# Sparse attention: turning and value products one step later, coefficients ahead of the masked minima

## The chip, the cores and the metric

One core of a Trainium2 chip. The metric is the device time of one launch in microseconds (us). The engines are PE (TensorE, matrix products and transposes, into the eight PSUM banks), DVE (VectorE), ACT (ScalarE), POOL (GpSimd) and SP, which here only issues the loads. Each engine works through its own program in order, and they meet by semaphores.

## The reference, cut to what matters

Two transformer layers, a third block with context, and an expert layer, for 256 tokens of width 1024. The change lies in the sparse attention of the second layer (`nsa_mixer`): 16 heads of width 64 in 4 key groups, three branches. With 256 tokens there are only four blocks of 64 keys, so the branch that selects blocks takes all of them, and the window of 256 holds every earlier key. Two branches are therefore plain causal attention over 256 keys, each with its own keys and values:

```python
ss = jnp.einsum('bqgrd,bgqkd->bgrqk', qb, k_sel)
p_slc = masked_softmax(ss, sel_mask)
o_slc = jnp.einsum('bgrqk,bgqkd->bqgrd', p_slc.astype(v_sel.dtype), v_sel)
sw = jnp.einsum('bqgrd,bkgd->bgrqk', qb, k_win)
p_win = masked_softmax(sw, win_mask)
o_win = jnp.einsum('bgrqk,bkgd->bqgrd', p_win.astype(v_win.dtype), v_win)
out = gb[..., 0:1] * o_cmp + gb[..., 1:2] * o_slc + gb[..., 2:3] * o_win
```

The third branch, over 15 compressed keys, is made before the loop; its product with its values is added inside it.

## The kernel before, in words

All weights stream through a ring of six raw tiles of 1 MB; ACT copies each to a high part (`make_high`, L407), POOL subtracts to get the low part (L421), and PE multiplies three times for each product (L480, L481, L482). Nearly the whole kernel is such products.

The attention takes 16 steps (`NS`): eight pairs of heads by two branches, `steps[n] = (c, br)`. One step n goes through these stations:

- scores(n), PE, L1773: eight products of queries and keys into banks 4 and 5. It waits for `masked` of step n - 1, which says that the banks have been read.
- minima(n), DVE, L2035: four operations that add the causal mask, write to buffer `SB[n % 4]` and leave the row minimum of the negated scores. The last sets `masked`.
- exps(n), ACT, L1894: four exponentials in place in SB, with their row sums. They wait for `masked` of n.
- coefs(n), DVE, L2017 and L2019: the reciprocal of the sums, and its product with the gate. They wait for the exponentials of n.
- scale(n), POOL, L1673: four multiplications of SB by the coefficient, after coefs(n). Before it POOL makes, in steps 2 to 13, a quarter of a weight tile's low part (L444).
- turn(n), PE, L1801: six transposes of SB into banks 6 and 7. It waits for scale(n), and for both copies of turn n - 1.
- copies(n): ACT (L1921) takes bank 6 to `PT[n % 2]`, DVE (L2044) bank 7. They wait for turn(n) and for values(n - 2).
- values(n), PE, L1818: eight products with the values; in even steps L1811 goes ahead (the compressed branch, two products).

The order on each engine is written out by hand. The first three scores, minima and exponentials lie beside the projection of the values (`between` at L1789), which ends with a wait of PE for all of its products (`flush`, L1790). Then the loops run: PE at n does scores(n), turn(n - 2), values(n - 3); DVE does minima(n), coefs(n - 1), its copy(n - 2); ACT does exps(n), its copy(n - 2), and makes a high part of a weight tile ahead of the exponentials at n = 3 and n = 8; after its copy it splits finished outputs (`o_high`, L1910) at n = 8, 12, 16, and DVE (`o_low`, L2024) at n = 9, 13, 17. After the loop PE goes on with the output projection (`cols_product`, L1830), whose tiles are ready.

Of the kernel before, what the change touches and what calls it, by code (L numbers as in the profile page):

```python
# [20 lines left out]
ACT = mybir.ActivationFunctionType  # L21
# [95 lines left out]
class Modulation:  # L117
# [37 lines left out]
    def turn(self, pe, j, bank, row):  # L155

        pe.wait_ge(*self.copied.at(j + 1))
        for c in range(4):
            last = self.k.nc.tensor.matmul(bank[:, 2 * c:2 * c + 2], row[:, c * P:(c + 1) * P], self.pick, start=True, stop=True)  # L159
        last.then_inc(self.turned.sem, 1)  # L160
# [111 lines left out]
class Kernel:  # L272
# [1324 lines left out]
    def nsa(self):  # L1597
# [3 lines left out]
        nc, ps, G = self.nc, self.psum, G_NSA  # L1601
        v_, s_ = nc.vector, nc.scalar
# [25 lines left out]
        PT = [work(f"PT{i}", 768).rearrange("p (b n) -> p b n", b=2) for i in range(2)]  # L1628
# [10 lines left out]
        sco, masked, sexp, scoef, sscale, stn, spa, spd, spv, ohigh, olow = self.counters(  # L1639
            "at_scores", "at_masked", "at_exp", "at_coef", "at_scaled", "at_turned", "at_PT_act", "at_PT_dve", "at_values",  # L1640
            "at_o_high", "at_o_low")
# [7 lines left out]
        NS = len(steps)  # L1649
# [28 lines left out]
        def _(pe):  # L1678
# [84 lines left out]
            def scores(n):  # L1763
                c, br = steps[n]
                if n:
                    pe.wait_ge(*masked.at(n))
                else:
                    pe.wait_ge(*fd.at(20))
                    pe.wait_ge(*rready.at(1))
                for t in range(TT):  # L1770
                    for b in range(2):
                        rows = slice(64 * b, 64 * b + 64)
                        last = nc.tensor.matmul(ps[4 + b][:, 0:P] if t == 0 else ps[4 + b][:, P:384],  # L1773
                                                qT[rows, c, t * P:(t + 1) * P], kT[br][rows, c // 4, 0:(t + 1) * P],
                                                start=True, stop=True)
                last.then_inc(sco.sem, 1)
# [15 lines left out]
            def turn(n):  # L1792
                pe.wait_ge(*sscale.at(n + 1))
                if n:
                    pe.wait_ge(*spa.at(n))
                    pe.wait_ge(*spd.at(n))
                else:
                    pe.wait_ge(*cpte.at(1))
                for b in range(2):
                    for j in range(3):  # L1800
                        last = nc.tensor.transpose(ps[6 + b][:, j * P:(j + 1) * P], SB[n % 4][:, b, j * P:(j + 1) * P], self.ident)  # L1801
                last.then_inc(stn.sem, 1)

            def values(n):
                c, br = steps[n]
                o = ps[c // 2][:, (c % 2) * T:(c % 2 + 1) * T]
                if n == 0:
                    pe.wait_ge(*vbd.at(2))
                    pe.wait_ge(*vready.at(2))
                if br == 0:  # L1810
                    nc.tensor.matmul(o, Vbd[:, c // 4, 2 * (c % 4):2 * (c % 4) + 2, :].rearrange("p h d -> p (h d)"),  # L1811
                                     cPT[:, c // 4, :], start=c % 2 == 0, stop=True, skip_group_check=True)
                pe.wait_ge(*spa.at(n + 1))
                pe.wait_ge(*spd.at(n + 1))
                for t in range(TT):
                    for b in range(2):
                        col = br * 256 + (2 * (c // 4) + b) * 64
                        last = nc.tensor.matmul(o[64 * b:64 * b + 64, t * P:T], vv[:, t, col:col + 64],  # L1818
                                                PT[n % 2][:, b, 0:T] if t == 0 else PT[n % 2][:, b, T:384],
                                                start=False, stop=True, skip_group_check=True)  # L1820
                last.then_inc(spv.sem, 1)

            for n in range(2, NS + 3):
                if 3 <= n < NS:
                    scores(n)
                if 2 <= n < NS + 2:
                    turn(n - 2)
                if n >= 3:
                    values(n - 3)
            self.cols_product(pe, G, 16, self.xT, KD, 4, olow)  # L1830

        @self.block.scalar
        def _(act):
# [53 lines left out]
            def exps(n):  # L1887
                act.wait_ge(*masked.at(n + 1))
                if n >= 4:
                    act.wait_ge(*scoef.at(n - 3))  # L1890
                for b in range(2):
                    for t, cut in enumerate((slice(0, P), slice(P, 384))):
                        w = SB[n % 4][:, b, cut]
                        last = s_.activation(w, w, ACT.Exp, scale=-1.0, bias=nm[n % 4][:, 2 * t + b:2 * t + b + 1],  # L1894
                                             accum_out=sums[n % 4][:, 2 * t + b:2 * t + b + 1])
                last.then_inc(sexp.sem, 1)
# [10 lines left out]
            def o_high(j):  # L1907
                act.wait_ge(*spv.at(4 * j + 4))
                for k in (2 * j, 2 * j + 1):
                    s_.activation(self.xT[0][:, k, :], ps[j][:, (k % 2) * T:(k % 2 + 1) * T], ACT.Copy).then_inc(ohigh.sem, 1)  # L1910

            for n in range(NS + 2):
                if n in (3, 8):
                    self.make_high(act, G + 16 + (n + 2) // 5)
                if 3 <= n < NS:
                    exps(n)
                if n >= 2:
                    act.wait_ge(*stn.at(n - 1))
                    if n >= 4:
                        act.wait_ge(*spv.at(n - 3))  # L1920
                    s_.activation(PT[n % 2][:, 0, :], ps[6][:, 0:384], ACT.Copy).then_inc(spa.sem, 1)  # L1921
                if n >= 8 and n % 4 == 0:
                    o_high(n // 4 - 2)
            o_high(3)
# [4 lines left out]
        def _(dve):  # L1929
# [82 lines left out]
            def coefs(n):  # L2012
                c, br = steps[n]
                dve.wait_ge(*sexp.at(n + 1))
                if n >= 4:
                    dve.wait_ge(*sscale.at(n - 3))
                link(v_.reciprocal(coef[n % 4], sums[n % 4]))  # L2017
                o = coef[n % 4].rearrange("p (t b) -> p t b", t=TT)
                v_.tensor_tensor(o, o, gates[:, :, 2 * c:2 * c + 2, 1 + br], ALU.mult).then_inc(scoef.sem, 1)  # L2019

            def o_low(j):
                dve.wait_ge(*ohigh.at(2 * j + 2))
                for k in (2 * j, 2 * j + 1):
                    v_.tensor_tensor(self.xT[1][:, k, :], ps[j][:, (k % 2) * T:(k % 2 + 1) * T],  # L2024
                                     self.xT[0][:, k, :].bitcast(F32), ALU.subtract).then_inc(olow.sem, 1)

            for n in range(NS + 2):
                if n < NS:
                    dve.wait_ge(*sco.at(n + 1))
                    if n >= 4:  # L2030
                        dve.wait_ge(*stn.at(n - 3))
                        dve.wait_ge(*sexp.at(n - 3))
                    for b in range(2):
                        for t, cut in enumerate((slice(0, P), slice(P, 384))):
                            last = v_.tensor_tensor_reduce(SB[n % 4][:, b, cut], ps[4 + b][:, cut], causal[:, cut], -SC, 3.0e38,  # L2035
                                                           ALU.add, ALU.min, nm[n % 4][:, 2 * t + b:2 * t + b + 1])
                    last.then_inc(masked.sem, 1)
                if 1 <= n < NS + 1:
                    coefs(n - 1)
                if n >= 2:  # L2040
                    dve.wait_ge(*stn.at(n - 1))
                    if n >= 4:
                        dve.wait_ge(*spv.at(n - 3))
                    v_.tensor_copy(PT[n % 2][:, 1, :], ps[7][:, 0:384]).then_inc(spd.sem, 1)  # L2044
                if n >= 9 and n % 4 == 1:
                    o_low(n // 4 - 2)
            o_low(3)
# [1280 lines left out]
```

## Time and profile before

| | us |
|---|---|
| median of three runs | 2133.19 |
| lowest, highest | 2129.83, 2133.97 |
| the profiled execution | 2131.12 |
| its span | 2129.3 |
| PE busy in the span | 2100.2 (99%) |
| POOL busy | 1654.5 (78%) |
| ACT busy | 1116.4 (52%) |
| DVE busy | 880.1 (41%) |
| TensorE's granted clock | 0.998 of full speed |

Rows of the timeline give the start in us from the beginning of the span, the busy time, the engine, the line of the kernel, the operation and its operands; in brackets stands the idle time before it and what the profile takes to have ended it. An instruction's busy time can overlap the start of the next one on the same engine, so the distance of two starts is what one costs in a row of work.

### The profile page before, as it was taken

To read this page: it belongs to the slowest core of one execution; us is meant where nothing else is said; L and a number is where in the kernel's file an instruction comes from. 1 tells how busy PE (TensorE), PEld (TensorE's weight loads), DVE (VectorE), ACT (ScalarE), POOL (GpSimd) and SP (SyncE) were. 2 spreads that over 40 slices of the span, in tenths; PEclk is the share of its full clock that TensorE was granted. 3 is DMA by queue.
4 is the path that set the end of the run, shared out by engine and by line. 5 is a ranking of instruction groups with operands and counts; after the bars stand their busy time and mean duration, and the time that the engine had idled before them with its cause. 6 is when DMAs were issued, how large, how long until landed. Compare 5 with 4: busy or idle time off the path is not lost.

```text
span 2129.3 us, 39500 instructions
## 1 busy us (share of the span) xinstructions
PE 2100.2 (99%) x15948; PEld 1972.1 (93%) x15948; DVE 880.1 (41%) x1921; ACT 1116.4 (52%) x1784; POOL 1654.5 (78%) x811
## 2 busy tenths in 40 slices
PE   9999999999999998999999999999999999999998
PEld 9999889999999986999989999999999998888886
DVE  6114633114112434411746315997667512322224
ACT  6455765435444446544654545555554455555555
POOL 5887667887888556888766576797676789999997
PEclk9999999999999999999999999999999999999999
DMA  8555666556555431655453355355444455555554
GB/s 306 198 181 195 258 237 257 197 197 251 196 197 186 170 139 62 219 181 196 177 191 139 139 178 208 110 191 167 140 149 140 149 177 195 197 194 196 191 196 149
DMA packets 77586, 393.70 MB, mean 185 GB/s; under 512 B 10749, under 2 KB 11901, under 8 KB 46849
## 3 DMA queue, kind: packets, MB, share of 16 engines
q1 hardware_dynamic: 77440, 391.70, 52.1%
q8 instruction: 99, 1.62, 0.3%
q14 instruction: 47, 0.38, 0.1%
HBM read 390.62 MB, written 1.05 MB: 184 GB/s over the span
## 4 chain that ended last, share of the span: by engine, by line
PE 84%; DVE 2%; ACT 1%; POOL 1%; issue 1%; DMA 0%; ACTq 0%; SPq 0%; DVEq 0%; POOLq 0%
PE bank L480 25%; PE bank L482 25%; PE bank L481 25%; PE bank L960 3%; PE bank L2717 3%; POOL nsa_SB L1673 1%; DMA ring_raw<-in_stream 0%; PE bank L1773 0%; PE bank L1801 0%; PE bank L147 0%; PE bank L1818 0%; DVE nsa_SB L2035 0%; PE bank L159 0%; DVE keep_red L2424 0%; ACT ring_high L407 0%
## 5 line engine op out<-in xcount | busy, mean ns | idle before, releaser
L421 POOL TENSOR_TENSOR ring_low<-ring_raw,ring_high 128x2048 fp32r<-128x2048 f32 x204 | 944.1, 4640 | 330.4 <-ACT ring_high L407 329.5
L2677 POOL TENSOR_TENSOR peerS_low<-peerS_raw,peerS_high 128x512 fp32r<-128x512 f32 x510 | 662.8, 1319 | 113.0 <-ACT peerS_high L2821 111.2
L480 PE MATMUL bank<-keep_xThigh,ring_high 128*128 128x256 f32 x2112 | 591.9, 280 | 5.0 <-POOL ring_low L421 1.5
L481 PE MATMUL bank<-keep_xTlow,ring_high 128*128 128x256 f32 x2112 | 585.7, 277 | 0.0
L482 PE MATMUL bank<-keep_xThigh,ring_low 128*128 128x256 f32 x2112 | 585.6, 277 | 0.0
L407 ACT ACTIVATE ring_high<-ring_raw 128x2048 fp32r<-128x2048 f32 x207 | 396.8, 1917 | 279.8 <-PE bank L482 247.6
L2821 ACT ACTIVATE peerS_high<-peerS_raw 128x512 fp32r<-128x512 f32 x510 | 319.5, 627 | 175.3 <-PE bank L482 150.4
L480 PEld LDWEIGHTS bank<-keep_xThigh,ring_high 128*128 128x128 f32 x2112 | 397.6, 188 | 13.5 <-issue 6.6
L481 PEld LDWEIGHTS bank<-keep_xTlow,ring_high 128*128 128x128 f32 x2112 | 398.0, 188 | 0.4
L482 PEld LDWEIGHTS bank<-keep_xThigh,ring_low 128*128 128x128 f32 x2112 | 397.8, 188 | 0.0
L480 PE MATMUL bank<-keep_xThigh,peerS_high 128*128 128x256 f32 x1024 | 292.0, 285 | 0.1
L481 PE MATMUL bank<-keep_xTlow,peerS_high 128*128 128x256 f32 x1024 | 285.9, 279 | 0.0
L482 PE MATMUL bank<-keep_xThigh,peerS_low 128*128 128x256 f32 x1024 | 285.7, 279 | 0.0
L921 DVE TENSOR_TENSOR bank<-bank,keep_R 128x512 f32<-128x512 f32 x44 | 30.8, 700 | 423.7 <-PE bank L482 423.5
L3043 DVE TENSOR_TENSOR peerS_GAlow<-peerA_A,peerS_GAhigh 128x256 fp32r<-128x256 f32 x127 | 98.2, 774 | 245.3 <-ACT peerS_GAhigh L2846 245.3
L480 PE MATMUL bank<-peerS_high,peerS_GAhigh 128*128 128x512 f32 x508 | 197.7, 389 | 0.6 <-DVE peerG_GA3low L3043 0.6
L481 PE MATMUL bank<-peerS_low,peerS_GAhigh 128*128 128x512 f32 x508 | 197.6, 389 | 0.0
L482 PE MATMUL bank<-peerS_high,peerS_GAlow 128*128 128x512 f32 x508 | 197.6, 389 | 0.0
L480 PEld LDWEIGHTS bank<-keep_xThigh,peerS_high 128*128 128x128 f32 x1024 | 193.1, 189 | 0.6 <-PE bank L960 0.2
L481 PEld LDWEIGHTS bank<-keep_xTlow,peerS_high 128*128 128x128 f32 x1024 | 193.6, 189 | 0.0
L482 PEld LDWEIGHTS bank<-keep_xThigh,peerS_low 128*128 128x128 f32 x1024 | 192.9, 188 | 0.0
L480 PEld LDWEIGHTS bank<-peerS_high,peerS_GAhigh 128*128 128x128 f32 x508 | 95.3, 188 | 20.7 <-DVE peerG_GA3low L3043 1.0
(549 smaller groups left out, 3546.8 us busy)
## 6 DMA issues: line engine op xcount, KB each, us to landing
ring_raw<-in_stream SPq DMA_DIRECT2D x237, 1024.0 KB, 4.8
peerS_raw<-in_experts SPq DMA_DIRECT2D x256, 512.0 KB, 3.7
start_x<-in_x SPq DMA_DIRECT2D x2, 512.0 KB, 4.0
ring_raw<-in_stream SPq DMA_DIRECT2D x4, 256.0 KB, 5.5
context_in<-in_ctx SPq DMA_DIRECT2D x1, 1024.0 KB
mix_band_band<-in_band SPq DMA_DIRECT2D x1, 1024.0 KB, 7.4
peerT_keys_keys<-in_stream SPq DMA_DIRECT2D x1, 1024.0 KB, 4.8
out<-keep_x SPq DMA_DIRECT2D x4, 256.0 KB, 2.2
```

The lines of the kernel that those rows point to most:

```text
L407: self.nc.scalar.activation(self.parts(n)[0], self.raw_slot(n), ACT.Copy).then_inc(self.high_done.sem, 1)
L421: self.nc.gpsimd.tensor_tensor(low_, self.raw_slot(n), high.bitcast(F32), ALU.subtract).then_inc(self.low_done.sem, 1)
L480: mm(out, sh, mh, start=start, stop=False)
L481: mm(out, sh, ml, start=False, stop=False)
L482: return mm(out, sl, mh, start=False, stop=stop)
L921: v_.tensor_tensor(pair(i, 0), pair(i, 0), over, ALU.mult).then_inc(scaled.sem, 1)
L960: ins = self.nc.tensor.matmul(out, lhsT, rhs, start=start, stop=stop)
L1673: last = g_.tensor_scalar(w, w, coef[n % 4][:, 2 * t + b:2 * t + b + 1], 1.0, ALU.mult, ALU.mult)
L2677: g_.tensor_tensor(low[:, m % 2, cut], xraw[:, m % 3, cut], high[:, m % 2, cut].bitcast(F32), ALU.subtract).then_inc(made_low.sem, 1)
L2717: last = nc.tensor.matmul(ps[2 + q % 2][:, j * P:(j + 1) * P], O1[:, o, :], O2[:, o, :], start=True, stop=True)
L2821: s_.activation(halves_of(m, 0)[:, cut], xraw[:, m % 3, cut], ACT.Copy).then_inc(made_high.sem, 1)
L3043: v_.tensor_tensor(cell(1, n), A[:, n, :], cell(0, n).bitcast(F32), ALU.subtract).then_inc(gal.sem, 1)
```

## The change

The loop of PE runs scores(n), turn(n - 3), values(n - 4), from n = 3 to NS + 3. ACT runs exps(n), copy(n - 3), from n = 3. DVE runs coefs(n - 1) first, then minima(n), then copy(n - 3). The buffers, the instructions of each station, their number, and POOL's program stay as they are. The first turn, which stood ahead of scores(3), now stands behind it.

```diff
-            for n in range(2, NS + 3):
-                if 3 <= n < NS:
+
+            for n in range(3, NS + 4):
+                if n < NS:
                     scores(n)
-                if 2 <= n < NS + 2:
-                    turn(n - 2)
-                if n >= 3:
-                    values(n - 3)
+                if n < NS + 3:
+                    turn(n - 3)
+                if n >= 4:
+                    values(n - 4)
...
-            for n in range(NS + 2):
+            for n in range(3, NS + 3):
                 if n in (3, 8):
                     self.make_high(act, G + 16 + (n + 2) // 5)
-                if 3 <= n < NS:
+                if n < NS:
                     exps(n)
-                if n >= 2:
-                    act.wait_ge(*stn.at(n - 1))
-                    if n >= 4:
-                        act.wait_ge(*spv.at(n - 3))
-                    s_.activation(PT[n % 2][:, 0, :], ps[6][:, 0:384], ACT.Copy).then_inc(spa.sem, 1)
+                m = n - 3
+                act.wait_ge(*stn.at(m + 1))
+                if m >= 2:
+                    act.wait_ge(*spv.at(m - 1))
+                s_.activation(PT[m % 2][:, 0, :], ps[6][:, 0:384], ACT.Copy).then_inc(spa.sem, 1)
...
-            for n in range(NS + 2):
+            for n in range(NS + 3):
+                if 1 <= n < NS + 1:
+                    coefs(n - 1)
                 if n < NS:
                     dve.wait_ge(*sco.at(n + 1))
...
                     last.then_inc(masked.sem, 1)
-                if 1 <= n < NS + 1:
-                    coefs(n - 1)
-                if n >= 2:
-                    dve.wait_ge(*stn.at(n - 1))
-                    if n >= 4:
-                        dve.wait_ge(*spv.at(n - 3))
-                    v_.tensor_copy(PT[n % 2][:, 1, :], ps[7][:, 0:384]).then_inc(spd.sem, 1)
+                if n >= 3:
+                    m = n - 3
+                    dve.wait_ge(*stn.at(m + 1))
+                    if m >= 2:
+                        dve.wait_ge(*spv.at(m - 1))
+                    v_.tensor_copy(PT[m % 2][:, 1, :], ps[7][:, 0:384]).then_inc(spd.sem, 1)
```

## Rows read from the trace of the kernel before

**Rows 1.** Waits of PE over the span: engine line waited for: us, times, longest.
```profile
PE bank L1801 <- POOL nsa_SB L1673: 7.8, 10, 1.4
```

**Rows 2.** Windows: the loop from scores(4) to scores(15), busy time of each engine.
```profile
792.78:828.28 35.50, 29.54 (x254) 19.47 (x253) 24.21 (x126) 26.81 (x103) 31.29 (x55) 1.00 0.17 61
```

**Rows 3.** Timeline of PE: scores(10), turn(9), values(8), scores(12), turn(11).
```profile
812.71 0.93 PE L1773 MATMUL bank<-nsa_kT,nsa_qT 64*128 64x128 f32 x8
...
817.25 0.85 PE L1801 MATMUL bank<-keep_ident,nsa_SB 128*128 128x128 f32 x6 [1.16 <-POOL nsa_SB L1673]
...
818.46 0.87 PE L1818 MATMUL bank<-nsa_PT,nsa_vv 128*64 128x256 f32 x8
819.26 0.93 PE L1773 MATMUL bank<-nsa_kT,nsa_qT 64*128 64x128 f32 x8
...
823.81 0.85 PE L1801 MATMUL bank<-keep_ident,nsa_SB 128*128 128x128 f32 x6 [1.16 <-POOL nsa_SB L1673]
```

**Rows 4.** Timeline of POOL: scale(9), a quarter, scale(11).
```profile
815.27 1.63 POOL L1673 TENSOR_SCALAR nsa_SB<-nsa_SB,nsa_coef 128x128 f32<-128x128 f32 x4 [0.96 <-DVE nsa_coef L2019]
816.87 1.27 POOL L444 TENSOR_TENSOR ring_low<-ring_raw,ring_high 128x512 fp32r<-128x512 f32 x1
...
821.82 1.63 POOL L1673 TENSOR_SCALAR nsa_SB<-nsa_SB,nsa_coef 128x128 f32<-128x128 f32 x4 [0.68 <-DVE nsa_coef L2019]
```

**Rows 5.** Timeline of ACT: first of exps(10), copy(8), copy(10).
```profile
814.92 0.40 ACT L1894 ACTIVATE nsa_SB<-nsa_SB,nsa_nm 128x128 f32<-128x128 f32 x1 [1.65 <-DVE nsa_nm L2035]
...
816.69 0.47 ACT L1921 ACTIVATE nsa_PT<-bank 128x384 f32<-128x384 f32 x1
...
823.24 0.47 ACT L1921 ACTIVATE nsa_PT<-bank 128x384 f32<-128x384 f32 x1
```

**Rows 6.** Timeline of all engines: minima(15), turn(13), exps(15), coefs(15).
```profile
829.25 0.29 DVE L2035 CUSTOM_DVE_ANT_0 nsa_SB<-bank,nsac_causal 128x128 f32<-128x128 f32 x1 [0.50 <-PE bank L1773]
...
830.37 0.85 PE L1801 MATMUL bank<-keep_ident,nsa_SB 128*128 128x128 f32 x6 [1.16 <-POOL nsa_SB L1673]
...
830.49 0.40 ACT L1894 ACTIVATE nsa_SB<-nsa_SB,nsa_nm 128x128 f32<-128x128 f32 x1 [0.22 <-DVE nsa_nm L2035]
...
832.38 0.18 DVE L2017 RECIPROCAL nsa_coef<-nsa_sums 128x4 f32<-128x4 f32 x1 [0.58 <-ACT nsa_SB L1894]
```

**Rows 7.** Timeline of DVE: coefs(9)'s reciprocal, copy(8), the product of coefs(10).
```profile
814.80 0.17 DVE L2017 RECIPROCAL nsa_coef<-nsa_sums 128x4 f32<-128x4 f32 x1
...
815.09 0.55 DVE L2044 COPY nsa_PT<-bank 128x384 f32<-128x384 f32 x1
...
817.47 0.70 DVE L2019 TENSOR_TENSOR nsa_coef<-nsa_coef,nsa_gates 128x4 f32<-128x4 f32 x1
```

**Rows 8.** Timeline of ACT from the loop's start: copy(0), high part, exps(3), exps(4).
```profile
790.03 0.47 ACT L1921 ACTIVATE nsa_PT<-bank 128x384 f32<-128x384 f32 x1
790.40 1.90 ACT L407 ACTIVATE ring_high<-ring_raw 128x2048 fp32r<-128x2048 f32 x1
792.20 0.39 ACT L1894 ACTIVATE nsa_SB<-nsa_SB,nsa_nm 128x128 f32<-128x128 f32 x1
...
794.99 0.40 ACT L1894 ACTIVATE nsa_SB<-nsa_SB,nsa_nm 128x128 f32<-128x128 f32 x1 [0.56 <-DVE nsa_nm L2035]
```

**Rows 9.** Timeline of PE: turn(0), the first work behind the flush.
```profile
789.11 0.84 PE L1801 MATMUL bank<-keep_ident,nsa_SB 128*128 128x128 f32 x6 [0.30 <-POOL nsa_SB L1673]
```

**Rows 10.** Timeline from turn(14) to the output projection: turn, values(13), copy(14), turn(15), projection.
```profile
832.82 0.85 PE L1801 MATMUL bank<-keep_ident,nsa_SB 128*128 128x128 f32 x6 [0.38 <-POOL nsa_SB L1673]
...
833.60 0.87 PE L1818 MATMUL bank<-nsa_PT,nsa_vv 128*64 128x256 f32 x8
833.71 0.50 ACT L1921 ACTIVATE nsa_PT<-bank 128x384 f32<-128x384 f32 x1 [0.98 <-PE bank L1801]
...
834.54 0.88 PE L1801 MATMUL bank<-keep_ident,nsa_SB 128*128 128x128 f32 x6
...
837.23 0.38 PE L480 MATMUL bank<-keep_xThigh,ring_high 128*128 128x256 f32 x1
```

## The prediction

> **What bounds the kernel now.** The page comes first: PE is busy for 99% of the span, at full clock, so a change can only give back time in which PE stands idle. The list of PE's waits says where that is: the longest entry of the whole span is the turns of this attention, 7.8 us in ten waits, put down to POOL's scaling [rows 1]. The waits behind the attention are short handovers right behind PE's own work, which move along with PE; so what the loop loses or wins stays in the total. The window of the loop then gives the pace: 35.50 us from scores(4) to scores(15), eleven steps, 3.23 us each, with PE busy 29.54 of it [rows 2].
>
> Next the timeline of the loop, engine by engine, to see what a turn really waits for. The profile names POOL. Turn(9) starts at 817.25, scale(9) was over at 815.27 + 1.63 = 816.90, a gap of 0.35; turn(11) starts at 823.81, 0.36 behind scale(11) [rows 3, 4]. A turn also waits until ACT has emptied bank 6, and copy(8) ends at 816.69 + 0.47 = 817.16, copy(10) at 823.24 + 0.47 = 823.71, both 0.09 to 0.10 before the turns [rows 5]. So the turn is released by ACT's copy, and that copy is late because it is queued on ACT behind exps(n). The loop's period is this circle over two steps: scores(10) at 812.71; exps(10) at 814.92 (2.21: scores, minima); copy(8) at 816.69 (1.77: four exponentials); turn(9) at 817.25 (0.56); turn, compressed product and values until scores(12) at 819.26 (2.01). Together 6.55 us for two steps [rows 3, 5].
>
> **The change part by part.** No station gains or loses an instruction. Three things move.
>
> *Turn and values one step later.* PE at n + 1 now runs turn(n - 2) where it ran turn(n - 1). It waits for copy(n - 3), and ACT runs that copy behind exps(n), as copy(n - 2) before. The circle scores(n), minima(n), exps(n), copy, turn, values, scores(n + 2) keeps every member: 6.55 us for two steps. scale gets a step more of lead, but it was not what the turns waited for. Value in the loop: nothing.
>
> *coefs(n - 1) ahead of minima(n) on DVE.* coefs(n - 1) waits for all exponentials of n - 1, and those wait for the last minimum of n - 1. Before, this wait stood behind minima(n), and minima(n) could run beside exps(n - 1). Now what is queued behind the waiting instruction is minima(n), and for it wait exps(n) and, through `masked`, scores(n + 1). That closes a new circle over one step: from the first exponential to the reciprocal 832.38 - 830.49 = 1.89; from the reciprocal through the product to the next DVE operation 815.09 - 814.80 = 0.29; from the first minimum to the first exponential 830.49 - 829.25 = 1.24 [rows 6, 7]. Sum 3.42 us. No row has minima behind coefs; the nearest is the copy behind coefs, the 0.29. The minima wait for one semaphore more, so I take 0.03 more, 3.45, with 3.42 and 3.50 as ends. Two steps then take 6.90, more than the old circle's 6.55, so the new circle rules and the old one has 0.35 of slack in two steps. PE's work is hidden in it. The DVE copy and `o_low` lie in the 1.89 in which DVE waits for ACT.
>
> At n = 8 ACT makes a high part of a weight tile between its copy and the exponentials. From first exponential to copy 1.77, to the high part 790.40 - 790.03 = 0.37, through it 792.20 - 790.40 = 1.80: 3.94 instead of 3.45, so 0.49 more once [rows 5, 8].
>
> *The start.* PE's first work behind the flush starts at 789.11 [rows 9]; it is now scores(3) instead of turn(0), so exps(3) could start at 789.11 + 2.21 = 791.32. But ACT makes the high part first, now without copy(0) ahead of it: 790.03 + 1.80 = 791.83 [rows 8]. That rules. exps(4) follows at 791.83 + 3.45 = 795.28, against 794.99: 0.29 later.
>
> *The end.* From exps(4) to exps(15) it was 830.49 - 794.99 = 35.50; it becomes 11 x 3.45 + 0.49 = 38.44: 2.94 later [rows 6, 8]. From exps(15) to the output projection it was 837.23 - 830.49 = 6.74 [rows 6, 10]. Now one turn and one values more are left at that point. copy(12) runs at 1.77 after exps(15) begins, turn(13) at 1.77 + 0.56 = 2.33; turn(13), compressed product and values(12) take 2.01: 4.34; turn(14) 833.60 - 832.82 = 0.78 and values(13) 819.26 - 818.46 = 0.80: turn(15) at 5.92; from there to the projection 837.23 - 834.54 = 2.69: 8.61 [rows 3, 10]. copy(14) doesn't hold turn(15) up: it can begin 833.71 - 832.82 = 0.89 behind turn(14), at 5.23, and takes 0.50. scale(15) is over at 1.89 + 0.47 + 1.63 = 3.99 (the 0.47 from the reciprocal to scaling is 815.27 - 814.80) [rows 4, 7]. The tail is 8.61 - 6.74 = 1.87 longer.
>
> **Sum:** 0.29 + 2.94 + 1.87 = +5.1 us. The profiled execution took 2131.12 (span 2129.3 and 1.8 around it), so 2136.2 for its like. It lies 2.1 below the median of the runs, 2133.19; on the median the sum is 2138.3. That is what I predict.
>
> *A lock between DVE and POOL.* The product of coefs(10) took 0.70 us, where its fellows take 0.17, and ended at 818.17; POOL's quarter ran from 816.87 to 818.14 [rows 4, 7]. So it was held until the quarter was over. This matters more now, since coefs is on the circle. The Trainium skill has a rule for it (page "SBUF — State Buffer", section "SBUF: two separate sides"): VectorE operations with two SBUF inputs and GpSimd operations take a shared port as an exclusive lock for the whole instruction. By that rule any overlap would lengthen the circle, and the rival below prices it; the trace agrees by that row. Where does the quarter fall? Counted from the first exponential, scaling begins at 1.89 + 0.47 = 2.36, the quarter at 2.36 + 1.60 = 3.96, and it is over at 5.23; the next reciprocal begins at 3.45 + 1.89 = 5.34 [rows 4, 6]. It misses by 0.1, and since POOL starts from coefs the two stay in step. I take nothing for it; the upper end is 0.53 in each of ten steps, 5.3 us.
>
> **The rivals.**
> *B, the new circle is hidden.* If the minima were still released by their scores, the pace would stay 3.23 and only start and tail count: 0.29 + 1.87 = +2.2, 2135.4. For it: DVE idles much in the loop (24.21 of 35.50 busy, rows 2). Against it: exps(10) to coefs and minima is a strict order of waits.
> *C, the page is right and POOL is the bound; faster.* Turn(n - 3) finds its scaling long done and the 7.8 us of PE's waits go [rows 1]; less the tail, 7.8 - 1.9 = 5.9 us faster, 2127.3. It decides from the point where a step takes under 3.03 us: 0.29 + 11p - 35.50 + 1.87 = 0 gives p = 3.03. Against it: exponentials and minima alone, 1.89 + 1.24 = 3.13, stand above that, and the copies meet the turns to 0.1 us.
> *D, the lock.* Up to 5.3 us on top: 2143.6. For it the 0.70; against it the order worked out above.
> That the later turn doesn't do what it says is part of the forecast: the lead it gives to POOL goes unused, because the copy stays behind exps.
>
> **How the numbers follow.** Forecast 0.68, B 0.13, C 0.08, D 0.11. What a measurement tells from no change is about 0.2%, 4.3 us. The forecast's +5.1 lies just above; its own spread (3.42 to 3.50 a step is -0.3 to +0.6 us, and three runs before spread over 4.1 us) puts some 0.28 of it below: 0.49 slower, 0.19 within. With B within, D slower and C faster: slower 0.60, same 0.32, faster 0.08. The range 2133.5 to 2143.0 holds B, the forecast and most of D's smaller sizes, and leaves out C.
>
> **What would show it.** Right: DVE's reciprocals (L2017) idle before each for ACT, about 1.3 us in nearly every step (1.89 less the copy), where before one did; first exponentials 3.45 us apart; the quarters at n = 4 to 13 leave L2019 at 0.17; the projection starts near 842.3. Wrong: waits for PE's scores still ahead of the minima, or steps under 3.2 us; a step near 3.45 with the projection before 840 would mean that the tail is wrong.

## The result, and the profile after

| | before | changed |
|---|---|---|
| median, us (six runs each) | 2132.06 | 2140.84 |
| lowest, highest | 2129.83, 2133.97 | 2138.88, 2146.34 |
| ratio, 95% interval | | 1.0039, 1.0024 to 1.0054 |
| the profiled execution | 2131.12 | 2146.34 |
| PE's first work behind the flush to the projection | 48.12 | 56.91 |

The change makes the kernel slower, by 8.8 us on the medians; the forecast said 5.1. The profiled execution of the changed kernel is the slowest of its six, and 4.5 us of its distance lie ahead of the attention loop, where nothing was changed. Of these, 1.7 are a fall of TensorE's granted clock to 0.50 from 762.2 to 765.6, where the trace before stays at 1.00: from the first L960 product behind its wait of 0.49 us to the loop it is 793.62 - 760.38 = 33.24 against 789.11 - 757.57 = 31.54. So the stretch itself is the measure: from the first PE work behind the flush to the output projection. It was 789.11 to 837.23 [rows 9, 10] and is 793.62 to 850.53, 8.79 us longer.

PE's waits in the changed kernel. The turns are still on top, in place of the 7.8 us of [rows 1]. "issue" means that the profile shows no releaser; in all of them ACT's copy of the turn before ended 0.10 us ahead:

```profile
PE bank L1801 <- issue: 10.7, 11, 2.1
PE bank L1801 <- ACT nsa_PT L1922: 1.8, 1, 1.8
```

One step of the new circle (a closed chain of waits, in which each waits for the one before it), from the timeline of DVE and ACT: reciprocal, product, first minimum, first exponential, next reciprocal. It answers to [rows 6, 7].

```profile
827.90 0.18 DVE L2018 RECIPROCAL nsa_coef<-nsa_sums 128x4 f32<-128x4 f32 x1 [1.46 <-ACT nsa_SB L1895]
828.11 0.16 DVE L2020 TENSOR_TENSOR nsa_coef<-nsa_coef,nsa_gates 128x4 f32<-128x4 f32 x1
828.26 0.29 DVE L2038 CUSTOM_DVE_ANT_0 nsa_SB<-bank,nsac_causal 128x128 f32<-128x128 f32 x1
...
829.49 0.40 ACT L1895 ACTIVATE nsa_SB<-nsa_SB,nsa_nm 128x128 f32<-128x128 f32 x1 [1.25 <-DVE nsa_nm L2038]
...
831.39 0.18 DVE L2018 RECIPROCAL nsa_coef<-nsa_sums 128x4 f32<-128x4 f32 x1 [1.46 <-ACT nsa_SB L1895]
```

831.39 - 827.90 = 3.49 us, and DVE stands idle for 1.46 ahead of both reciprocals. Where the minima follow coefs the distance from the reciprocal to the next operation is 0.36, not the 0.29 + 0.03 that the forecast took. Now the first exponentials of steps 4, 5 and 15 ("step 4" is below the time from exps(4) to exps(5)):

```profile
799.98 0.40 ACT L1895 ACTIVATE nsa_SB<-nsa_SB,nsa_nm 128x128 f32<-128x128 f32 x1 [1.26 <-DVE nsa_nm L2038]
...
804.62 0.40 ACT L1895 ACTIVATE nsa_SB<-nsa_SB,nsa_nm 128x128 f32<-128x128 f32 x1 [2.41 <-DVE nsa_nm L2038]
...
840.32 0.40 ACT L1895 ACTIVATE nsa_SB<-nsa_SB,nsa_nm 128x128 f32<-128x128 f32 x1 [1.25 <-DVE nsa_nm L2038]
```

Step 4 takes 4.64 instead of 3.49, and the tail from exps(15) to the projection at 850.53 takes 10.21 instead of the 8.61 of the forecast. The reason stands in PE's timeline behind the two longest waits:

```profile
798.82 0.85 PE L1801 MATMUL bank<-keep_ident,nsa_SB 128*128 128x128 f32 x6 [2.06 <-issue]
...
800.23 1.55 PE L1818 MATMUL bank<-nsa_PT,nsa_vv 128*64 128x256 f32 x8
801.71 1.63 PE L1773 MATMUL bank<-nsa_kT,nsa_qT 64*128 64x128 f32 x8
...
842.65 0.85 PE L1801 MATMUL bank<-keep_ident,nsa_SB 128*128 128x128 f32 x6 [1.84 <-ACT nsa_PT L1922]
...
845.11 1.54 PE L1801 MATMUL bank<-keep_ident,nsa_SB 128*128 128x128 f32 x6
```

Eight values took 0.87 us before [rows 3] and take 1.55, eight scores 1.63 instead of 0.93. The windows give TensorE's granted clock (the third number from the end):

```profile
798.00:800.00 2.00, 1.18 (x8) 0.91 (x8) 1.59 (x11) 0.74 (x4) 1.15 (x3) 0.94 0.00 0
800.00:801.00 1.00, 1.00 (x5) 0.53 (x6) 0.42 (x1) 1.00 (x5) 1.00 (x3) 0.50 0.00 0
...
844.00:845.00 1.00, 1.00 (x8) 0.52 (x6) 0.09 (x1) 0.58 (x3) 0.31 (x1) 0.57 0.00 0
845.00:846.00 1.00, 1.00 (x6) 0.90 (x5) 0.00 (x0) 0.00 (x0) 0.00 (x0) 0.50 0.00 0
```

It fell to 0.50, its lower level of 1.2 GHz, and was back at 1.00 in the window from 804. A mean of 0.94 over two us means that it fell 0.24 us before 800.00, so at 799.8, about 1.0 us after PE had taken up work again behind a wait of 2.06 us. By the same working the second fall, at 844.1, came 1.5 us after the end of the wait of 1.84 us. Before the change it was 1.00 throughout the loop [rows 2].

### The profile page after: what moved, and what is told of

It reads as the page before. It is cut to its first block, busy times and chain, and to the rows that moved or that the text cites. A ratio compares the mean times of both kernels' runs of the same rounds, so it can differ in the third digit from the quotient of the medians.

```text
span 2144.5 us, 39500 instructions
## 1 busy us (share of the span) xinstructions
PE 2106.6 (98%) x15948; PEld 1975.8 (92%) x15948; DVE 869.8 (41%) x1921; ACT 1117.3 (52%) x1784; POOL 1651.0 (77%) x811
## 4 chain that ended last, share of the span: by engine, by line
PE 72%; POOL 6%; issue 3%; DVE 2%; ACT 2%; DMA 0%; ACTq 0%; POOLq 0%; DVEq 0%
PE bank L480 22%; PE bank L482 22%; PE bank L481 22%; POOL ring_low L421 6%; PE bank L2719 3%; PE bank L960 3%; ACT nsa_SB L1895 1%; DVE nsa_SB L2038 0%; ACT ring_high L407 0%; DMA ring_raw<-in_stream 0%; PE bank L1773 0%; PE bank L1818 0%; DVE keep_red L2426 0%; PE bank L1801 0%; DVE context_red L2426 0%
## 5 line engine op out<-in xcount | busy, mean ns | idle before, releaser
L3045 DVE TENSOR_TENSOR peerS_GAlow<-peerA_A,peerS_GAhigh 128x256 fp32r<-128x256 f32 x127 | 89.5, 706 | 254.0 <-ACT peerS_GAhigh L2848 254.0
```

Source lines behind the costliest of these rows:

```text
L3045: v_.tensor_tensor(cell(1, n), A[:, n, :], cell(0, n).bitcast(F32), ALU.subtract).then_inc(gal.sem, 1)
```

## The experiments

Each time is set beside the kernel before, run on the same chip. "Stretch" is from PE's first work behind the flush to the projection, "exps" from the first exponential of step 4 to that of step 15, both from one trace of each kernel. How well such a trace repeats is seen from the two kernels that were traced twice: their stretches differ by 0.06 and 0.01 us.

| kernel | ratio to before, 95% interval | stretch | exps |
|---|---|---|---|
| before | | 48.12 | 35.50 |
| changed | 1.0039, 1.0024 to 1.0054 | 56.91 | 40.34 |
| later turn only | 1.0017, 1.0008 to 1.0026 | 52.15 | 38.51 |
| coefs ahead only | 1.0018, 1.0009 to 1.0027 | 52.14 | 38.84 |
| long fillers | 1.0037, 1.0025 to 1.0049 | 55.66 | 39.82 |
| half of the scaling | 1.0003, 0.9994 to 1.0012 | 47.98 | 35.50 |
| copy first | 0.9981, 0.9969 to 0.9993 | 44.47 | 31.96 |
| changed, copy first | 1.0022, 1.0010 to 1.0034 | 53.09 | 39.20 |
| copy first, fewer quarters | 0.9967, 0.9952 to 0.9981 | 43.26 | 30.71 |
| short fillers | 1.0026, 1.0015 to 1.0037 | 54.20 | 39.19 |
| changed again | 1.0035, 1.0023 to 1.0048 | 56.97 | 40.38 |
| short fillers again | 1.0025, 1.0012 to 1.0038 | 54.21 | 39.21 |
| before, copy first | 1.0000, 0.9988 to 1.0011 | 47.41 | 34.38 |

### Does POOL release the turns?

```diff
# the kernel before, POOL
-                for b in range(2):
+                for b in range(1):
```

> The kernel before with half of POOL's scaling left out: two of the four multiplications in each step (the second head's rows stay unscaled), so scale(n) takes 0.8 us less. Theory (the turns are released by ACT's copy): the turns stay 0.09 to 0.10 behind ACT's copies, the pace stays 6.55 us in two steps, time as before within 0.5 us. Rival (POOL's scaling releases the turns, as the profile says): each of the ten waits shrinks by up to 0.8 us, 6 to 8 us faster.

The stretch stays, 47.98 against 48.12, and the eleven steps take 35.50 to the hundredth. PE's waits for the turns, a scaling, ACT's copy and the turn in this kernel:

```profile
PE bank L1801 <- issue: 7.5, 9, 1.4
```

```profile
816.81 0.83 POOL L1673 TENSOR_SCALAR nsa_SB<-nsa_SB,nsa_coef 128x128 f32<-128x128 f32 x2 [2.28 <-DVE nsa_coef L2019]
...
818.23 0.47 ACT L1921 ACTIVATE nsa_PT<-bank 128x384 f32<-128x384 f32 x1
...
818.79 0.85 PE L1801 MATMUL bank<-keep_ident,nsa_SB 128*128 128x128 f32 x6 [1.16 <-issue]
```

The scaling is over at 817.64 and the turn starts 1.15 us later, again 0.09 behind the copy's end at 818.70. The waits add up to 7.5 us, where each was to shrink by up to 0.8. The rival is out: the profile put the 7.8 us down to an engine that was already done.

### Which part costs what?

```diff
# later turn only: the changed kernel, DVE's loop
-                if 1 <= n < NS + 1:
-                    coefs(n - 1)
                 if n < NS:
                     (minima)
+                if 1 <= n < NS + 1:
+                    coefs(n - 1)
```

> The later turn alone: turn and values one step later as in the changed kernel, but coefs(n - 1) behind minima(n) again, as in the kernel before. Theory (the turns wait for ACT's copy, which stays queued behind the exponentials): the loop keeps its pace of about 3.25 us a step, the first exponentials again 6.55 us apart in two steps, and only start and tail are paid for: 1.9 us of tail, and up to 2.7 us if TensorE's clock falls at the two long waits as it did in the changed kernel (1.15 us in step 5, 1.6 us in the tail). So 2 to 4.5 us slower than before. Rival (the turns wait for POOL's scaling, as the profile says): the lead of one step takes the waits of 7.8 us away, so about 6 us faster than before.

Slower than before by 4.0 us in the stretch, 0.17% in the total; the rival's 6 us of gain are excluded. The tail is 841.99 - 833.35 = 8.64 (forecast 8.61). The steps from 5 to 15 take 3.28 us each: the old circle, unbroken. Step 4 takes 5.71. About 1.3 us of it are the clock, which was at half speed behind the wait for turn(1): from turn(1) to scores(5) and on to exps(5) it takes 2.57 + 2.94, where the rows of before have 2.01 + 2.21. By this estimate the later turn without the clock costs 2.7 us of the stretch. The two waits and their windows:

```profile
795.04 0.85 PE L1801 MATMUL bank<-keep_ident,nsa_SB 128*128 128x128 f32 x6 [2.06 <-ACT nsa_PT L1922]
...
835.68 0.84 PE L1801 MATMUL bank<-keep_ident,nsa_SB 128*128 128x128 f32 x6 [2.01 <-ACT nsa_PT L1922]
```

```profile
796.00:799.00 3.00, 3.00 (x18) 1.61 (x16) 0.48 (x1) 1.06 (x5) 2.21 (x4) 0.57 0.00 0
834.00:842.00 8.00, 6.32 (x55) 4.42 (x55) 2.75 (x8) 3.61 (x12) 2.94 (x8) 1.00 0.04 16
```

Behind the second wait, of 2.01 us, it did not fall. A difference of 0.05 us between two waits is little to decide it, and in a part that all kernels here share the clock fell in some executions and not in others (see the last section), so the length of the wait alone is not what decides.

```diff
# coefs ahead only: the kernel before, DVE's loop
+                if 1 <= n < NS + 1:
+                    coefs(n - 1)
                 if n < NS:
                     (minima)
-                if 1 <= n < NS + 1:
-                    coefs(n - 1)
```

> The order of DVE alone: coefs(n - 1) ahead of minima(n), turn and values two and three steps behind as before. Theory (a circle minima, exponentials, coefs, minima): the first exponentials stand 3.49 us apart in nearly every step, as in the changed kernel, so 11 x 3.49 + 0.44 = 38.8 us from exps(4) to exps(15) instead of 35.5; the tail stays as before; 3.3 us slower than before, and no step in which TensorE's clock falls. Rival (the order is hidden behind the scores): pace 3.23 us, no difference from before.

38.84 us for the eleven steps against 38.8 expected. exps(4), exps(5) and exps(15):

```profile
801.52 0.40 ACT L1894 ACTIVATE nsa_SB<-nsa_SB,nsa_nm 128x128 f32<-128x128 f32 x1 [1.25 <-DVE nsa_nm L2037]
...
805.01 0.40 ACT L1894 ACTIVATE nsa_SB<-nsa_SB,nsa_nm 128x128 f32<-128x128 f32 x1 [1.25 <-DVE nsa_nm L2037]
...
840.36 0.40 ACT L1894 ACTIVATE nsa_SB<-nsa_SB,nsa_nm 128x128 f32<-128x128 f32 x1 [1.26 <-DVE nsa_nm L2037]
```

The first two are 3.49 apart. The tail is 6.73, as before; the rest of its 4.0 us is 0.69 at the start, since minima(4) wait for exps(3), which stand behind the high part on ACT. Each half alone costs 4.0 us of the stretch; the change with both costs 8.8.

### Is the rest the clock?

```diff
# the changed kernel, PE's loop, ahead of turn(n - 3)
+                if n in (4, 16):
+                    for _ in range(14 if n == 4 else 12):     # short fillers: 8 and 7
+                        nc.tensor.matmul(ps[3 if n == 4 else 0][:, 0:P], self.ones, self.ones, start=True, stop=True)
```

> The changed kernel with idle time of TensorE filled: 14 products of 128x128 that nobody reads ahead of turn(1), 12 ahead of turn(13), the two places where it waited 2.06 and 1.84 us and its granted clock fell behind them. Theory (what the sum missed is mostly the clock): granted clock 1.00 through the loop, step 5 takes 3.49 us instead of 4.64, the tail is 1.6 us shorter; 2.75 us faster than the changed kernel, so some 6 us slower than before. Rival (the slow products come from something else, such as PSUM banks that other engines read): the products behind these waits stay at twice their time and the total stays at the changed kernel's, 8.8 us over before.

The clock stayed at 1.00, but the 14 fillers took 3.39 us, 0.24 each, and ended after the wait would have: the stretch fell by 1.25 only, step 4 took 4.12. The direction was right, the size not; the totals can't tell it from the changed kernel.

> The changed kernel with fillers that end before the waits do: 8 unread products ahead of turn(1), 7 ahead of turn(13) (a product of 128x128 took 0.24 us in the longer version, whose 14 and 12 ended 0.6 to 0.9 us behind the waits). Theory (clock): full clock through the loop, nothing delayed, first work behind the flush to projection 54.2 us instead of 56.9; 2.7 us faster than the changed kernel, 6 us slower than before. Rival (the clock was not the cause, or falls in spite of the filling): 56.9 us, as the changed kernel.

54.20, as expected, and the steps take 3.49 from the first on, but for the high part at n = 8 and the 0.36 ahead of minima(13). To have all on one chip, the changed kernel and this one once more:

> The changed kernel once more, to have it on one chip beside the two others of this call. Theory: 8 to 9 us slower than before (ratio near 1.0040), a wait of about 2 us ahead of turn(1) and of about 1.8 us ahead of turn(13), and a granted clock of 0.50 behind both, as in its first trace; 56.9 us from the first work behind the flush to the projection. Rival (the fall of the clock was an accident of the one profiled execution): clock 1.00 throughout, 54.2 us.

> The changed kernel with the short fillers (8 and 7 unread products) once more, on the same chip as the changed kernel itself. Theory (clock): 54.2 us from flush to projection, clock 1.00, total 2.7 us below the changed kernel of this call, some 6 us over before. Rival (the clock costs nothing in the total): the same total as the changed kernel.

56.97 and 54.21. The windows of the changed kernel again, behind turn(1) and turn(13), and then the one with short fillers over the whole loop:

```profile
800.00:804.00 4.00, 3.82 (x18) 2.50 (x20) 2.21 (x12) 2.31 (x10) 3.15 (x6) 0.57 0.00 0
844.00:848.00 4.00, 3.94 (x20) 2.61 (x21) 0.56 (x1) 1.04 (x3) 1.62 (x4) 0.59 0.00 0
```

```profile
790.00:850.00 60.00, 50.12 (x415) 35.47 (x414) 30.75 (x156) 39.24 (x140) 37.50 (x68) 1.00 0.16 54
```

So both falls recur, and keeping PE busy takes them away and 2.76 us with them. At full clock the change costs 6.1 us of the stretch. In the totals the medians are 2142.48 and 2140.55, 1.9 us apart, and the intervals of the two ratios overlap: that the gain reaches the whole run is likely, not shown.

### Cutting the circles

```diff
# copy first: later turn only, ACT's loop
-                if n < NS:
-                    exps(n)
                 (copy n - 3)
+                if n < NS:
+                    exps(n)
```

> The later turn without the new order of DVE, and ACT's copy(n - 3) ahead of exps(n) instead of behind it. Theory (the old circle closes through the copy that is queued behind the exponentials): with the copy ahead, the circle is cut, no wait of PE passes 1.5 us, its clock stays at full, and the bound becomes POOL's own work, 1.63 + 1.27 and the gap, 2.95 to 3.0 us a step, until the quarters end. Start and tail as before or 0.4 us shorter. Sum: 11 x 2.95 instead of 35.5, so 3 to 3.5 us faster than before. Rival (the copy only looks like the releaser, the turns wait for something that a copy in another place doesn't move, such as the scores): pace 3.23 as before, and with the longer tail 2 us slower than before.

44.47 us and faster than before. Against the kernel with the later turn only, this moves nothing but the copy ahead of the exponentials, so the circle that the turns were caught in did go through ACT's queue. The steps from 4 to 15 take 2.91 us, and what bounds them is worth a look. POOL's quarter and DVE's product of coefs:

```profile
807.99 1.27 POOL L444 TENSOR_TENSOR ring_low<-ring_raw,ring_high 128x512 fp32r<-128x512 f32 x1
```

```profile
808.22 1.07 DVE L2020 TENSOR_TENSOR nsa_coef<-nsa_coef,nsa_gates 128x4 f32<-128x4 f32 x1
809.21 0.54 DVE L2046 COPY nsa_PT<-bank 128x384 f32<-128x384 f32 x1
```

The product takes 1.07 instead of 0.17 and ends at 809.29, with the quarter (809.26): the lock that the forecast weighed. DVE's copy and the turn behind it come later by it. What it costs by itself was not measured: POOL has next to no gap in these steps, from scaling to scaling it is 809.38 - 806.39 = 2.99 us, so its own work bounds them.

> The changed kernel with ACT's copy(n - 3) ahead of exps(n). Theory (two circles, of which the new one through DVE's order rules): the first exponentials stay 3.49 us apart, since the copy is over before the minima are; but turn(1) and turn(13) no longer wait behind exponentials, so the clock doesn't fall and the longer tail goes. 3.49 x 11 instead of 35.5 leaves 2.5 to 3.3 us slower than before, 5 to 6 us faster than the changed kernel. Rival (one circle only, and it goes through the copy): pace falls to 3.0 us or less, faster than before.

```profile
PE bank L1773 <- DVE nsa_nm L2038: 9.9, 12, 1.4
```

With the old circle cut and the new one left, the exponentials stay 3.49 apart, and PE's wait moves to the scores, which stand for `masked`. Two circles, and the change's own is the slower one. The stretch is 3.8 us shorter than the changed kernel's, less than the 5 to 6 expected: the start is 0.85 longer than before (789.39 to exps(4) at 796.12), the tail 0.42, where turn(13) waits 1.52 us (the profile names POOL, but the scaling had ended 3.56 us before, DVE's copy 0.15 before), and the steps hold the 0.36 ahead of minima(13) again.

> As the one with the copy first and DVE's old order, and POOL makes only two weight tiles' low parts inside the loop (quarters in steps 2 to 9); the third is made whole behind the last scaling, some 9 us before the projection needs it. Theory (POOL's 2.95 to 3.0 us a step bounds that version while quarters run): steps 10 to 15 fall to PE's own 2.67 us on average, another 1 to 1.5 us faster, 4 to 5 us faster than before. Rival (something else bounds those steps, or PE waits for the third low part): same time as the version with twelve quarters, or slower.

```profile
819.43 0.40 ACT L1895 ACTIVATE nsa_SB<-nsa_SB,nsa_nm 128x128 f32<-128x128 f32 x1 [0.28 <-DVE nsa_nm L2036]
...
832.80 0.40 ACT L1895 ACTIVATE nsa_SB<-nsa_SB,nsa_nm 128x128 f32<-128x128 f32 x1
```

(`if 2 <= n < 10` in place of 14 in POOL's loop.) From exps(10) to exps(15) it is 13.37 us, 2.67 a step, and PE is busy for 13.32 of them: its own work is the bound. The version is 0.33% below the kernel before and has the shortest stretch here, 1.2 us under copy first; in the totals the intervals of these two overlap.

> The kernel before with one thing moved: ACT's copy(n - 2) ahead of exps(n). Turn and values stay two and three steps behind, coefs behind the minima. Theory: the circle through the queued copy is cut, and now the turn really waits for POOL: scores, minima 0.97 + 1.20, coefs and its handover 0.47, scaling 1.63, turn and values 1.6 to 2.1: about 6.1 us for two steps instead of 6.55, 1.7 us faster than before (0 to 2.5). So this time the lead of a step is worth something: the version with the copy first and the later turn stays 1.5 us better. Rival (the later turn adds nothing even then): 3.2 us faster than before, like that version.

```profile
PE bank L1801 <- POOL nsa_SB L1673: 6.5, 10, 1.1
```

```profile
814.72 1.62 POOL L1673 TENSOR_SCALAR nsa_SB<-nsa_SB,nsa_coef 128x128 f32<-128x128 f32 x4 [0.44 <-DVE nsa_coef L2019]
...
816.39 0.88 PE L1801 MATMUL bank<-keep_ident,nsa_SB 128*128 128x128 f32 x6 [0.77 <-POOL nsa_SB L1673]
```

0.7 us shorter in the stretch, nothing measurable in the total; I had expected 1.7. The exponentials stand 34.38 / 11 = 3.13 apart, not 3.05. Now the turn really waits for POOL: this one starts 0.05 behind the scaling's end at 816.34, the turns from 2 to 15 all 0.05 to 0.06, while ACT's copies ended 0.96 to 1.90 before. And here a later turn does pay: 2.9 us of the stretch between this version and the one with copy first. The later turn was right in itself; it lacked the copy ahead of the exponentials.

## Why the prediction was right or wrong

- **What the turns wait for.** Right, shown twice: less scaling changes nothing, and the copy moved ahead takes 7.7 us from the stretch of the kernel with the later turn (52.15 to 44.47), about 1.3 of them the clock, which fell there and not here.
- **The later turn brings nothing in the loop.** Right: 3.28 us a step with it alone, where the circle of before gives 3.27.
- **The new circle.** Right in kind; 3.49 us, not 3.45, since a minimum behind coefs starts 0.36 behind the reciprocal and not 0.32. That is 0.4 us over eleven steps.
- **The high part at n = 8.** 3.93 us from exps(7) to exps(8), 3.94 expected.
- **The tail.** 1.90 us longer where the clock held (8.64 with the later turn alone), 1.87 expected; 3.47 longer in the changed kernel.
- **The lock as no cost.** Right for the changed kernel: its sixteen products of coefs took 0.16 to 0.17 us each.
- **The sum: +5.1 against 8.8.** The term that is missing is TensorE's clock. The step from exps(4) to exps(5) took 1.15 us more than 3.49 and the tail 1.60 more, 2.75 of the 3.7 us; the short fillers gave back 2.71 and 2.76. The forecast's order holds two waits of PE of about 2 us, and it put what the clock does behind them at nothing; all the rows it used were at full clock. The rest is the 0.4 of the circle, 0.2 at the start, and 0.36 once ahead of minima(13), where DVE's first minimum came 0.51 behind the product instead of 0.15, with no releaser in the profile. That gap stands in the traces of all versions with the later turn and coefs ahead, and not in the one with coefs ahead only; its cause stays open.
- **The range.** The total of 2140.84 lies inside 2133.5 to 2143.0, but this is in part luck: the room above the forecast had been left for the lock, which cost nothing, and the clock filled it. What was right is the direction and its two causes, the steps and the tail.

The sum of the changed kernel's stretch: 0.48 at the start, 4.84 in the steps (11 x 3.49 + 0.44 + 1.15 + 0.36 - 35.50), 3.47 in the tail: 8.79.

## What to carry to other kernels

Before giving a stage more lead, find the release to the hundredth: the gap from the end of each candidate to the start of the waiting instruction, over several rounds. The true one leaves a short and constant gap: about 0.10 behind ACT's copy, 0.15 behind DVE's and 0.06 behind POOL's scaling, whichever of them released the turn. The false one can look steady too: in the kernel before, POOL's gap was 0.35 in six of the ten waits, 0.25 to 0.62 in three and 4.25 in the first. So test it by making the candidate shorter. In an in-order queue a wait that is moved forward takes along everything behind it; write the circle of waits down and add it up before moving one. And count a long wait of TensorE twice, once for itself and once for the clock that may fall behind it.

## What the runs showed of the hardware

- TensorE's clock fell to 0.50 within a loop in which PE was never idle for more than 2.06 us at a time. It fell each time only after PE had taken up work again: 1.0 and 1.5 us after in the first trace of the changed kernel, 0.2 and 0.7 us after in the repeat (in turn(1), whose six transposes took 1.37 us), 1.4 us after with the later turn alone. The waits ahead were of 2.06 and 1.84 us; behind one of 2.01 it held. Waits in the loop of up to 1.52 us, one in nearly every step, left it at 1.00 in all traces.
- The fall is not the same from one execution to the next. In the part ahead of the loop, which all kernels here share, the clock fell 1.8 to 2.6 us behind a wait of 0.49 us at L960 in seven of the thirteen traces and held in six; from there to the loop it is 33.0 to 33.4 us with the fall and 31.4 to 31.7 without. Both falls of the changed kernel came in two traces of two, and none in three of three with fillers. What decides between them these runs don't show.
- A 128x4 product with both inputs in SBUF on DVE, 0.17 us alone, took 1.07 us beside a POOL operation with two inputs in SBUF (128x512, 1.27 us), and ended with it.
- An unread fp32 product of 128x128 cost 0.24 us at full clock and stands in the trace as two records.
